# A fused two-stack transformer block: weight slots split before the stage barrier, and expert rows fetched four ahead

## The reference, cut to what matters

```python
# first stack: 256 context tokens + 256 tokens, D_MODEL = 1024, two layers
mixer (attention) -> layer_norm -> moe -> layer_norm
# moe: 16 experts of D_EXPERT = 512, each token goes to its best two
g = einsum('...d,edf->...ef', h, w_gate)
u = einsum('...d,edf->...ef', h, w_up)
a = silu(g) * u * gates
y = einsum('...ef,efd->...d', a, w_down)
# second stack: 16 meta tokens + 256 tokens, four layers: fox, gla, gdn, fox mixers
h = h + mixer(rmsnorm(h)); h = h + swiglu(rmsnorm(h), w_gate_up, w_down)   # d_ff = 2816
```

## Time and profile before

| what | value |
|---|---|
| median of 3 executions | 3912.59 us |
| the profiled execution, its own time | 3919.4 us |
| span of its instructions | 3917.6 us |
| PE busy | 3098.7 us (79%) |
| DVE busy | 2201.0 us (56%) |
| ACT busy | 1618.9 us (41%) |
| mean granted TensorE clock | 0.88 |
| DMA | 524.39 MB, mean 134 GB/s |

### The profile page before, as it was taken

How to read it: one execution, slowest core, us unless ns; L and a number is a source line. 1 busy time by engine, 2 the same in 40 slices (tenths; PEclk the granted TensorE clock), 3 DMA queues, 4 the chain that set the end, 5 groups by cost and what they waited for, 6 DMA issues and landing times. The chain is left out here.

```text
span 3917.6 us, 55129 instructions
## 1 busy us (share of the span) xinstructions
PE 3098.7 (79%) x20792; PEld 2724.8 (70%) x20792; DVE 2201.0 (56%) x3823; ACT 1618.9 (41%) x2862; POOL 88.5 (2%) x82
## 2 busy tenths in 40 slices
PE   8996766988666999676799856999366589895798
PEld 3474546887545888674699846999256579793698
DVE  0026855877564888427666365664733456636666
ACT  1133534776444777434432424334231143334433
POOL 0000001101000111000000000000000000000000
PEclk9998987999787999887899958999658889996899
DMA  9820014999203999330154301554000035450153
GB/s 348 279 75 22 1 43 166 320 320 331 97 11 108 339 344 337 95 99 1 56 173 160 128 11 65 172 161 144 29 1 1 1 119 171 127 153 0 44 182 118
DMA packets 420933, 524.39 MB, mean 134 GB/s; under 512 B 14608, under 2 KB 387424, under 8 KB 420496
## 3 DMA queue, kind: packets, MB, share of 16 engines
q1 hardware_dynamic: 408400, 499.75, 39.0%
q0 software_dynamic: 9696, 12.70, 1.0%
q10 hardware_dynamic: 2656, 9.49, 0.6%
HBM read 521.81 MB, written 21.13 MB: 139 GB/s over the span
## 5 line engine op out<-in xcount | busy, mean ns | idle before, releaser
L1670 DVE TENSOR_TENSOR W_lo<-ring,W_hi 128x1024 fp32r<-128x1024 f32 x384 | 453.0, 1222 | 44.0 <-ACT W_hi L1588 43.4
L1211 PE MATMUL ps<-H_split_hi,W_hi 128*128 128x272 f32 (+1 forms) x1408 | 411.2, 292 | 49.3 <-DVE W_lo L1315 49.3
L501 PE MATMUL ps<-ACC_part,W_hi 128*128 128x272 f32 (+2 forms) x1624 | 351.8, 300 | 77.4 <-DVE ACC_part L542 44.9
L1212 PE MATMUL ps<-H_split_lo,W_hi 128*128 128x272 f32 (+1 forms) x1408 | 409.1, 291 | 0.0
L1213 PE MATMUL ps<-H_split_hi,W_lo 128*128 128x272 f32 (+1 forms) x1408 | 406.2, 288 | 0.0
L535 DVE TENSOR_TENSOR W_lo<-ring,W_hi 128x1024 fp32r<-128x1024 f32 x198 | 232.6, 1222 | 307.0 <-ACT W_hi L511 307.0
L1588 ACT ACTIVATE W_hi<-ring 128x1024 fp32r<-128x1024 f32 x384 | 384.7, 1052 | 41.6 <-PE ps L1504 20.7
L1315 DVE TENSOR_TENSOR W_lo<-ring,W_hi 128x1024 fp32r<-128x1024 f32 x264 | 313.6, 1221 | 142.6 <-ACT W_hi L1257 142.1
L501 PEld LDWEIGHTS ps<-ACC_part,W_hi 128*128 128x128 f32 x1624 | 269.9, 193 | 85.5 <-issue 79.8
L1257 ACT ACTIVATE W_hi<-ring 128x1024 fp32r<-128x1024 f32 x264 | 259.0, 1050 | 118.8 <-PE ps L1228 75.4
L1211 PEld LDWEIGHTS ps<-H_split_hi,W_hi 128*128 128x128 f32 x1408 | 268.0, 190 | 50.9 <-issue 50.9
(11 more groups left out here) (365 smaller groups left out, 6911.6 us busy)
## 6 DMA issues: line engine op xcount, KB each, us to landing
ring<-in_w_down SPq DMA_DIRECT2D x108, 1024.0 KB, 5.5
ring<-in_w_gate_up SPq DMA_DIRECT2D x88, 1024.0 KB, 5.1
ring<-in_w_gate SPq DMA_DIRECT2D x64, 1024.0 KB, 5.5
ring<-in_w_up SPq DMA_DIRECT2D x64, 1024.0 KB, 6.0
ring<-in_w_mod SPq DMA_DIRECT2D x48, 1024.0 KB, 8.7
ring<-in_fox_w_in SPq DMA_DIRECT2D x32, 1024.0 KB, 6.0
ring<-in_gdn_w_in SPq DMA_DIRECT2D x16, 1024.0 KB, 5.6
ring<-in_gla_w_in SPq DMA_DIRECT2D x12, 1024.0 KB, 5.5
```

The source lines that it names most:

```text
L501: mm = pe.matmul(self.out(i), a, b, start=(k == 0 and n_part == 0), stop=(k == KC - 1 and n_part == 2))
L1211: pe.matmul(out, wh[:, k, M], Hh[:, k, X], start=(k == 0), stop=False)
L1212: pe.matmul(out, wh[:, k, M], Hl[:, k, X], start=False, stop=False)
L1670: dve.tensor_tensor(lo, c.ring[:, (self.g0 + p) % SLOTS, W], hi.bitcast(F32), ALU.subtract)\
```

## The change

Three things are changed.

1. `Stage` gets two new parts, `scalar_early` and `vector_early`, which `run` calls ahead of the barrier of the stage. In `Project`, `FeedForward` and (by inheritance) `Experts` they hold the split of the first three slots: all uppers of slots 0, 1, 2 on ACT, all lowers of the same on DVE. The places where these splits stood in the stage are removed. Other stages' early parts are empty.
2. POOL issues fetches 0 to 3 first, and in round e it issues fetch e + 4 instead of e + 2. The two row buffers and the waits inside `fetch` stay as they are. In the gathered path, steps 4 to 7 are taken out of the hardware loop on PE, ACT and DVE, which now runs five rounds over steps 8 to 27.
3. The `HeadNorm` behind the first attention uses columns of QK (no longer needed there) for its temporaries, in place of `s` and `p`, which overlap `W_hi`.

```diff
+    FIRST = (("G", 0), ("U", 0), ("G", 1))
+    def scalar_early(self, act):          # FeedForward, Experts
+        for kind, n in self.FIRST:
+            self.upper(act, kind, n)
+    def vector_early(self, dve):
+        for kind, n in self.FIRST:
+            self.lower(dve, kind, n)
...
+    def scalar_early(self, act):          # Project
+        for s in range(SPLIT_SLOTS):
+            self.upper(act, s)
+    def vector_early(self, dve):
+        for s in range(SPLIT_SLOTS):
+            self.lower(dve, s)
...
-        upper(0)
         for k in range(KC):
             act.activation(self.parts[0][k][:, T], self.src[:, k, T], ACT.Copy)\
                .then_inc(self.scalar_done, self.act.mark("src", k))
-        for s in range(1, SPLIT_SLOTS):
-            upper(s)
...
-        lower(0)
         for k in range(KC):
             dve.wait_ge(self.scalar_done, self.act.at("src", k))
...
-        for s in range(1, len(self.sources)):
-            lower(s)
+        for s in range(SPLIT_SLOTS, len(self.sources)):
+            self.lower(dve, s)
...
-        fetch(0)
-        fetch(1)
+        for e in range(4):
+            fetch(e)
         for e in range(EXPERTS):
-            if e + 2 < EXPERTS:
-                fetch(e + 2)
+            if e + 4 < EXPERTS:
+                fetch(e + 4)
...
-        for n in range(4):
+        for n in range(8):
             step(n)
-        with pe.Fori(0, N // 4 - 2) as i:
-            for n in range(4, 8):
+        with pe.Fori(0, N // 4 - 3) as i:
+            for n in range(8, 12):
                 step(n, i)
...
-                   SUBLN_EPS, m["s"], m["p"], after=1.0 - LAM_INIT)
+                   SUBLN_EPS, QK[:, 0:4, :], QK[:, 4:8, :], after=1.0 - LAM_INIT)
...
         def run(eng, part, early=None):
             for n, stage in enumerate(stages):
+                if early:
+                    early(stage, eng)
                 if n:
                     eng.wait_ge(core.stage_done, 3 * n)
                 part(stage, eng)
```

More of the change, by code:

```diff
@@ L359, in pool @@
         pass
+    def scalar_early(self, act):
+        pass
+    def vector_early(self, dve):
+        pass
 class Modulation(Stage):
@@ L502, in tensor, with upper, lower @@
             mm.then_inc(c.mm_done, 1)
+    def upper(self, act, s):
+        c = self.c
+        c.arrived(act, self.g0 + s)
+        for half in range(2):
+            W = slice(half * SLOT // 2, (half + 1) * SLOT // 2)
+            act.activation(self.slot_parts(s)[0][:, W], c.ring[:, (self.g0 + s) % SLOTS, W], ACT.Copy)\
+               .then_inc(c.hi_done, 1)
+    def lower(self, dve, s):
+        c = self.c
+        hi, lo = self.slot_parts(s)
+        for half in range(2):
+            W = slice(half * SLOT // 2, (half + 1) * SLOT // 2)
+            dve.wait_ge(c.hi_done, self.L0 + 2 * s + half + 1)
+            dve.tensor_tensor(lo[:, W], c.ring[:, (self.g0 + s) % SLOTS, W], hi[:, W].bitcast(F32), ALU.subtract)\
+               .then_inc(c.lo_done, 1)
+    def scalar_early(self, act):
[4 more added lines that the diff above has]
+            self.lower(dve, s)
     def scalar(self, act):
         c, T = self.c, slice(self.t0, self.t1)
[L507 to L512, removed]
-        upper(0)
         for k in range(KC):
@@ L524, in scalar @@
             if s + SPLIT_SLOTS < len(self.sources) and self.items[i + 1][0] != s:
-                upper(s + SPLIT_SLOTS)
+                self.upper(act, s + SPLIT_SLOTS)
     def vector(self, dve):
[L528 to L536, removed]
-        lower(0)
+        T = slice(self.t0, self.t1)
         for k in range(KC):
@@ L1243, in tensor, with upper, lower, scalar_early @@
         down(self.N - 1)
+    FIRST = (("G", 0), ("U", 0), ("G", 1))
+    def upper(self, act, kind, n, i=None):
+        c, p = self.c, self.pos(kind, n)
+        g = self.g0 + p
+        c.arrived(act, g, i)
+        if p >= SPLIT_SLOTS:
+            act.wait_ge(c.mm_done, self.at(self.through(p - SPLIT_SLOTS), i, 24))
+        for half in range(2):
+            C = slice(half * SLOT // 2, (half + 1) * SLOT // 2)
+            act.activation(self.parts(p)[0][:, C], c.ring[:, g % SLOTS, C], ACT.Copy).then_inc(c.hi_done, 1)
+    def lower(self, dve, kind, n, i=None, halves=(0, 1)):
+        c, p = self.c, self.pos(kind, n)
+        for half in halves:
+            C = slice(half * SLOT // 2, (half + 1) * SLOT // 2)
+            hi, lo = (w[:, C] for w in self.parts(p))
+            dve.wait_ge(c.hi_done, self.at(self.L0 + 2 * p + half + 1, i, 12))
+            dve.tensor_tensor(lo, c.ring[:, (self.g0 + p) % SLOTS, C], hi.bitcast(F32), ALU.subtract)\
+               .then_inc(c.lo_done, 1)
+    def scalar_early(self, act):
+        for kind, n in self.FIRST:
+            self.upper(act, kind, n)
+    def vector_early(self, dve):
+        for kind, n in self.FIRST:
+            self.lower(dve, kind, n)
     def scalar(self, act):
@@ L1248, in upper @@
         def upper(kind, n, i=None):
[L1249 to L1257, removed]
+            self.upper(act, kind, n, i)
         def silu(n, i=None):
@@ L1309, in lower @@
         def lower(kind, n, i=None, halves=(0, 1)):
[L1310 to L1316, removed]
+            self.lower(dve, kind, n, i, halves)
         def gated(n, i=None):
@@ L1630, in step @@
                 silu(n + 1, i)
-        upper("G", 0)
-        upper("U", 0)
         for e in range(2):
@@ L1640, in gathered_scalar @@
         silu(0)
-        for n in range(4):
+        for n in range(8):
             step(n)
-        with act.Fori(0, N // 4 - 2) as i:
-            for n in range(4, 8):
+        with act.Fori(0, N // 4 - 3) as i:
+            for n in range(8, 12):
                 step(n, i)
@@ L1705, in step @@
                 product(n + 1, i)
-        lower("G", 0)
-        lower("U", 0)
         for e in range(2):
@@ L1711, in gathered_vector @@
             xlo(e, 1)
-        lower("G", 1)
         lower("U", 1)
@@ L1715, in gathered_vector @@
         product(0)
-        for n in range(4):
+        for n in range(8):
             step(n)
-        with dve.Fori(0, N // 4 - 2) as i:
-            for n in range(4, 8):
+        with dve.Fori(0, N // 4 - 3) as i:
+            for n in range(8, 12):
                 step(n, i)
@@ L2557, in build, with run @@
         block = ctx.enter_context(nc.Block())
-        def run(eng, part):
+        def run(eng, part, early=None):
             for n, stage in enumerate(stages):
+                if early:
+                    early(stage, eng)
                 if n:
@@ L2577, in _ @@
         def _(act):
-            run(act, lambda stage, eng: stage.scalar(eng))
+            run(act, lambda stage, eng: stage.scalar(eng), lambda stage, eng: stage.scalar_early(eng))
         @block.vector
         def _(dve):
-            run(dve, lambda stage, eng: stage.vector(eng))
+            run(dve, lambda stage, eng: stage.vector(eng), lambda stage, eng: stage.vector_early(eng))
         @block.gpsimd
```

7 lines of the change are left out of this document (removed).

## The result

The changed kernel takes 3937.02 us in the median of seven executions (3933.58 to 3944.52), the kernel before in the same comparison 3917.58 (3911.95 to 3924.37, seven). The ratio is 1.005, its 95% interval 1.0038 to 1.0062: the change makes the kernel **19 us slower**, where +27 and 3940 were forecast. The profiled execution took 3940.8 us, its span is 3939.0.

A forecast was written before the change was run, and what follows sets the result against it. TensorE leads at 79% busy, its waits at weight-stage starts and for fetched rows being what the change touches. Starts +49 us and fetches -22 us give +27 on the 3912.6 us median, 3940 us; range 3922 to 3959.

The forecast's parts named there:

- Project starts: Twelve Projects: TensorE starts later behind the barrier; nine cost 30.6 us, three where ACT is last or just through 13.3 us.
- the short Zero: The Zero stage of 0.12 us; the Project behind it was forecast to lose 4.3 us.
- FeedForward starts: Four FeedForwards: TensorE starts 1943.4 instead of 1942.15, a loss of 1.3 us each, 5.2 us together.
- such shifts: Lower-clock stretches behind the sixteen starts move with the start's position, leaving some 5 us; starts given 42 to 55 us.
- Experts, head: Start of Experts: TensorE waits for fetched rows, so early splits there cost and save nothing.
- the row chain: Scatter, table and first fetch ahead of the two expert loops: 35.9 us of row waits, which the change leaves alone.
- Loops: Two expert loops: fetches ahead of writes remove 37.9 us of row waits; 17 + 5 = 22 us less, bounds 3 and 44.
- ceiling of 346 GB/s: DMA rate assumed for the new expert loops, midway between 340 and 352; the loops then take 292 and 284 us.
- Peel: Taking one round out of the expert loops costs nothing, bounds 0 to +2 us a loop.
- HeadNorm's new temporaries: HeadNorm's temporaries keep the same shapes in their new place: forecast to cost nothing.
- rival of loops with room: Expert loops: all row waits and the clock come back, 44 us; total 3918, no measurable change; chance 0.10.
- rival of starts truly ahead: Project and FeedForward: slots split before the barrier, TensorE starts 1.0 us behind it; 56 us less, total 3835; chance 0.05.

The follow-up runs named there:

- best: Changed kernel with ACT splitting only slot 0 early, DVE nothing, TensorE starting on hi-by-hi products, Experts' first lowers behind the route-table wait: 3840.67 us, ratio 0.9801.
- fetch_only: The kernel before with the new fetch order and the peeled round, no early splits: 3875.63 us, ratio 0.9905.
- lower_after_table: fetch_only with DVE's first lowers in Experts put behind the wait for the route table: 3874.76 us, ratio 0.9901 against the kernel before.
- peel_only: The kernel before with nothing but the peeled loop round (steps 4 to 7 outside the hardware loop): 3921.09 us, ratio 1.0009.
- extra_dma: fetch_only with 256 KB more DRAM-to-DRAM DMA beside every down-slot load in Experts: 3907.81 us, ratio 0.9976 against the kernel before.
- experts_late: The changed kernel, but Experts stages split nothing ahead of their barrier: 3935.16 us, ratio 1.0053 against the kernel before.
- act3_dve1: The changed kernel with three slots' uppers early on ACT but only slot 0's lower early on DVE: 3875.26 us, ratio 0.9898 against the kernel before.

## Why the prediction was right, and what in it was off

- **Project starts, +43.9 us forecast (30.6 + 13.3): right.** +44.0 by stage, +44.3 by waits. The place by place forecast of 7.4 us behind the barrier is 7.49 in the trace, 8.5 where ACT is last is 8.83 and 8.81, 8.3 behind the short Zero is 8.32. The two Projects of 512 tokens started at 7.74.
- **FeedForward starts, +5.2 us: right** by waits (+5.5), short by stage (+8.1). Most of the rest fits the clock: behind the starts these four stages spend 44.3 us at the lower clock where they spent 37.2, and 7 us at half speed are worth 3.5 by estimate. The range had 5 us for such shifts.
- **Experts, head, nothing forecast: wrong by 4.5 us.** The prediction called the early work hidden under the row chain. The time of the work was hidden, but not its effect on another engine: beside DVE's lowers POOL's issues in that very chain took up to twice as long, 2.8 us of the 4.5; the other 1.7 came with later landings whose cause stays open. This is the step whose mechanism was wrong, and the hint stood in the trace of before, where one scatter of the first layer takes 1.97 us, just while lowers run.
- **Loops, -22 us forecast: mis-sized.** Measured behind the heads: 361.0 to 335.3 and 332.7 to 320.4 us, -25.7 and -12.3, in sum -38.0. The mechanism was right (fetch ahead of the write, row waits gone, ACT waits on the ring in their place; some 7 of the 25.7 us are the clock, by estimate, with 31.6 us at the lower level behind the first head where there were 45.7), the term that failed is the ceiling of 346 GB/s: the loops ran at 354 and 357, and up to 365 with more to move. A DMA share of 1.00 was read as full, and it isn't: shares of 1.03 and 1.04 stand in the loops after, and the earlier trace rows had 1.10 in the modulation stage. The prediction took that stage's 348 GB/s as support for its 346; the 20 us before it in the same trace moved more, and so do 20 us of the changed kernel's first loop (columns as in the earlier trace rows):

```profile
20.00:40.00 20.00, 20.00 (x95) 7.88 (x93) 0.00 (x0) 2.19 (x6) 0.00 (x0) 1.00 1.08 369
```

```profile
700.00:720.00 20.00, 20.00 (x151) 18.95 (x150) 17.98 (x21) 16.31 (x22) 2.73 (x2) 1.00 1.07 371
```

The Trainium skill (DMA: Bandwidth & Descriptors, "Where 436 GB/s comes from") has some 358 GB/s for HBM-to-SBUF transfers; by that the prediction gave 41 us less, and over the whole loops the traces agree with it, at 354 to 357, better than with my midpoint; the two 20 us stretches above stand over it.
- **Peel, nothing: right** in the median (ratio 1.0009). HeadNorm's new temporaries: its stage took 19.66 us before and after.
- **The sum:** +43.9 + 5.2 + 0 - 22 = +27 forecast; +44.0 + 8.1 + 4.5 - 38.0 + 2.8 = +21.4 in the profiles, +19.4 in the medians. So the total is partly luck: the loops gave 16 us more than forecast, and the heads, FeedForward and the stages that weren't touched took 10 us of it back. It is luck too that 3940 is only 3 us off: the kernel before came out 5 us slower beside the changed one than in the three executions that the 27 us were added to. The low end of the range isn't the sum of its terms either: 42 less 35 is +7, not +10. The rival of loops with room came nearer in its term for the loops (44 forecast, 38 measured) than the forecast did, but not in its time for the whole (3918). The rival of starts truly ahead is excluded by the timeline of every start.

## What to carry to other kernels

In this kernel, putting work ahead of a barrier helped only on an engine that waits there, and only as much work as that engine's lead; on the engine that arrives last it stands in front of everything the next stage needs first, and must be cut to what the first matmul needs. So for each barrier write down when each engine arrives before moving anything, and move the pieces engine by engine: here three slots on both cost 52 us in the Project and FeedForward stages, one slot gave 16 us. A queue that serves two purposes (fetch and write) should hold first what waits for least; that alone gave 39 us.

## What the runs showed of the hardware that was not expected

- POOL's indirect DMAs beside VectorE. Alone, an issue takes 0.95 to 1.11 us. Of the 28 scatters in these twelve traces that lie wholly beside back-to-back lowers (subtractions with two SBUF operands, 128x1024, 1.22 us each), 16 take 1.83 to 1.97 us, one 1.43, and 11 only 0.96 to 1.09; no other scatter takes over 1.11. All 28 end 0.29 to 0.31 us before the end of a lower, which is about the gap to the next scatter, so the next one begins as that lower ends (in the changed kernel's second layer the fourth scatter begins at 1232.11, where the second lower ends). How long an issue gets thus depends on where it begins against DVE's instructions. In `best`, where the lowers meet the fetches instead, two fetches take 1.39 and 1.91 us (1.06 and 1.00 before). The Trainium skill (GPSIMD Engine Reference, "Specifications") says that GpSimd shares its SBUF interfaces with VectorE and names two SBUF inputs as a case of contention; these rows agree and give its size.
- TensorE has two paces at the same clock. In the three FeedForward stages of 272 tokens it keeps one of them behind the start: 126.6 ns a matmul or 124.4, with the granted clock at 1.00 and no wait. The same stretch of the third such stage, in the kernel before and in `fetch_only` (the same code there; 1266 and 1288 matmuls in 160 us):

```profile
3202.00:3362.00 160.00, 160.00 (x1266) 160.00 (x1265) 102.59 (x173) 58.90 (x71) 0.00 (x0) 1.00 0.52 171
```

```profile
3161.00:3321.00 160.00, 160.00 (x1288) 160.00 (x1288) 105.44 (x178) 58.97 (x71) 0.00 (x0) 1.00 0.53 175
```

  It makes 3.4 us a stage. The kernel before and the changed one run all three at the slower pace, so their difference is free of it; `fetch_only` and `lower_after_table` run two at the faster one, `peel_only`, `extra_dma`, `experts_late` and `act3_dve1` one, the others none. What chooses the pace stays open, and differences of 3 to 7 us between profiles of this kernel are to be read with it in mind.
- The profile's DMA share isn't bounded by 1: 1.03 to 1.04 over the new loops, with 354 to 365 GB/s.
